# Memory norm's row scale applied to the products instead of the rows, memory rows loaded in column pieces, identity transposes left out

## The reference, cut to what matters

```python
def rms_norm(x, g):
    xf = x.astype(jnp.float32)
    y = xf * lax.rsqrt(jnp.mean(xf * xf, axis=-1, keepdims=True) + RMS_EPS)
    return (y * g.astype(jnp.float32)).astype(x.dtype)

mem_n = rms_norm(mem, mem_norm_g)              # mem: (256, 2048)
for layer in range(DEPTH):                     # DEPTH = 2
    mem_kv = mem_n @ mem_w_kv[layer]           # (2048, 1024): 512 columns of k, 512 of v
```

## Time and profile before

| | |
|---|---|
| median of three runs | 2245.72 us |
| profiled execution, span | 2243.6 us |
| TensorE busy | 2210.5 us (99%) |
| VectorE, ScalarE, GpSimd busy | 46%, 37%, 18% |
| TensorE idle ahead of its first instruction | 8.44 us |
| first product | 13.77 us |
| first product of memv0, memk1, memv1 | 40.47, 62.26, 88.92 us |

### The profile page before, as it was taken

How to read it: one execution, slowest core, us unless ns; L and a number is a source line. 1 busy time by engine, 2 the same in 40 slices (tenths; PEclk the granted TensorE clock), 3 DMA queues, 4 the chain that set the end, 5 groups by cost and what they waited for, 6 DMA issues and landing times.

```text
span 2243.6 us, 30418 instructions
## 1 busy us (share of the span) xinstructions
PE 2210.5 (99%) x11723; PEld 1824.8 (81%) x11723; DVE 1022.6 (46%) x1909; ACT 824.6 (37%) x1481; POOL 408.8 (18%) x699
## 2 busy tenths in 40 slices
PE   8999999999999999999999999999999999999998
PEld 7888888888888788888888878888887878777886
DVE  5632456556532356643353441442112357666534
ACT  6532233333323444422342223322222455555323
POOL 1626112322221012200010111100000154221100
PEclk9999999999999999999999999999999999999999
DMA  8645444444446346563353447444533675554632
GB/s 292 202 141 135 127 130 122 130 147 124 119 120 199 114 138 223 172 218 97 113 165 106 143 150 232 131 132 146 160 112 98 200 234 183 174 183 148 213 98 94
DMA packets 167052, 345.65 MB, mean 154 GB/s; under 512 B 21663, under 2 KB 32239, under 8 KB 164483
## 3 DMA queue, kind: packets, MB, share of 16 engines
q1 hardware_dynamic: 106832, 188.51, 28.1%
q0 software_dynamic: 31376, 98.44, 13.6%
q10 hardware_dynamic: 28707, 56.84, 6.9%
HBM read 279.89 MB, written 63.83 MB: 153 GB/s over the span
## 4 chain that ended last, share of the span: by engine, by line
PE 96%; ACT 1%; issue 1%; DVE 1%; DMA 1%; POOL 0%; SPq 0%; ACTq 0%; DVEq 0%; POOLq 0%
PE PS L244 79%; PE PS L1841 3%; PE PS L1830 2%; PE PS L296 1%; PE PS L2012 1%; PE PS L2367 1%; PE PS L587 1%; PE PS L1574 1%; PE PS L2541 1%; PE PS L2156 1%; PE PS L2400 1%; PE PS L2543 1%; PE PS L2037 1%; PE PS L658 1%; ACT wsp L206 0%
## 5 line engine op out<-in xcount | busy, mean ns | idle before, releaser
L244 PE MATMUL PS<-A,wsp 128*128 128x512 f32 (+2 forms) x5136 | 1141.0, 383 | 2.7 <-DVE A L573 1.2
L244 PEld LDWEIGHTS PS<-A,wsp 128*128 128x128 f32 (+1 forms) x5136 | 933.8, 188 | 196.5 <-issue 6.8
L213 DVE TENSOR_TENSOR wsp<-wraw,wsp 128x1024 fp32r<-128x1024 f32 (+1 forms) x357 | 431.3, 1209 | 889.4 <-ACT wsp L206 888.3
L244 PE MATMUL PS<-wsp,A 128*128 128x512 f32 x2928 | 747.5, 400 | 3.7 <-DVE stage L1912 1.8
L206 ACT ACTIVATE wsp<-wraw 128x1024 fp32r<-128x1024 f32 (+1 forms) x357 | 372.0, 1045 | 898.8 <-PE PS L244 868.2
L244 PEld LDWEIGHTS PS<-wsp,A 128*128 128x128 f32 x2928 | 531.8, 188 | 105.9 <-issue 9.4
L349 ACT ACTIVATE stage<-PS 128x512 f32<-128x512 f32 (+1 forms) x150 | 85.8, 592 | 104.3 <-PE PS L244 99.8
L1877 ACT ACTIVATE S<-PS 128x256 f32<-128x256 f32 (+3 forms) x160 | 63.0, 394 | 118.9 <-PE PS L1830 118.1
L1885 ACT ACTIVATE S<-PS,stats 128x256 f32<-128x256 f32 (+3 forms) x160 | 75.0, 469 | 75.8 <-DVE stats L1922 64.3
L1841 PEld LDWEIGHTS PS<-S 128*128 128x128 f32 x640 | 93.0, 191 | 10.2 <-issue 1.1
L1841 PE MATMUL PS<-S 128*128 128x128 f32 x640 | 94.3, 274 | 0.6 <-issue 0.6
(11 more groups left out here) (370 smaller groups left out, 1763.9 us busy)
## 6 DMA issues: line engine op xcount, KB each, us to landing
wraw<-in_even_w_in_dram SPq DMA_DIRECT2D x112, 512.0 KB, 3.7
wraw<-in_odd_w_in_dram SPq DMA_DIRECT2D x88, 512.0 KB, 3.6
wraw<-in_w_out_dram SPq DMA_DIRECT2D x80, 512.0 KB, 3.7
wraw<-in_mem_w_kv_dram SPq DMA_DIRECT2D x32, 512.0 KB, 4.3
yO<-stage ACTq DMA_DIRECT2D x12, 1024.0 KB
yE<-stage ACTq DMA_DIRECT2D x10, 1024.0 KB
S<-yO POOLq DMA_DIRECT2D x36, 256.0 KB, 3.7
hA<-stage ACTq DMA_DIRECT2D x8, 1024.0 KB
```

Source lines behind the costliest of these rows:

```text
L213: nc.vector.tensor_tensor(wsp[:, q, 1, :, 0:j["cols"]], wraw[:, q, :, 0:j["cols"]], wsp[:, q, 0, :, 0:j["cols"]].bitcast(F32), ALU.subtrac ...
L244: mm = nc.tensor.matmul(dst, lhs, rhs, start=(s == 0 and kk == 0 and i == 0), stop=(s == j["spc"] - 1 and kk == 1 and i == 2))
```

## The change

Six things change, all in the first 115 us.

- The rows of `mem` are transposed as they are loaded, without a scale. The row factor `memR` is applied when the products leave PSUM: for memv0 and memv1 by ScalarE, as the scale of its copy (`act_evac_cols`), and for memk0 and memk1, where a row is a column of the result, by VectorE, which multiplies with a tile `memB` that has the 256 factors in every partition (`dve_evac_rows`). `memB` is made by two matmuls of a matrix of ones with two diagonal matrices (`dve_diag`, `pe_row_scales` in slot 7 between its 12th and 13th product, `dve_row_scales`).
- The squares of `mem` move behind the tiles of slots 3 and 4, the root behind those of slot 5.
- `mem` is loaded in five column pieces of both row tiles (256, 256, 512, 512 and 512 columns), each ahead of one weight slot.
- The gains are loaded by ScalarE's queue at its start instead of by POOL's.
- The 14 identity transposes are left out.
- The loads of x tiles 2 and 3 wait for the sixth transposed k tile; those of tiles 0 and 1 for the squares as well.

`dve_evac_rows` stands in VectorE's queue where `act_evac` stood in ScalarE's: in the next product, behind the splits of its first three slots. ScalarE keeps the store there, which waits for the four banks.

```diff
-        def dve_chunk(dve, j, c, hook=None, split=0):
+        def dve_chunk(dve, j, c, hook=None, split=0, pending=None):
             for s, n, q, r, early in chunk_slots(j, c):
+                if s == 3 and pending:
+                    pending()
                 if s >= split:
                     dve_slot(dve, j, n, q)
...
+        def dve_evac_rows(dve, j):
+
+            if j["stored0"]:
+                dve.wait_ge(stored, 16 * j["stored0"])
+            for f in range(4):
+                dve.wait_ge(*((bank_done, j["done0"] + f + 1) if f < 3 else (slot_used, j["slot0"] + j["spc"])))
+                dve.wait_ge(rb_ok, 1)
+                nc.vector.tensor_tensor(stage[:, f, 0:NMEM], PS[:, f, 0:NMEM], memB, ALU.mult).then_inc(banks_free, 1)
+
+        def act_evac_cols(act, j):
+
+            act.wait_ge(stored, 16 * j["stored0"])
+            act.wait_ge(rows_ok, 1)
+            for f in range(2):
+                act.wait_ge(*((bank_done, j["done0"] + 1) if f < 1 else (slot_used, j["slot0"] + j["spc"])))
+                nc.scalar.activation(stage[:, f, :], PS[:, f, :], ACT.Copy, scale=memR[:, f:f + 1]).then_inc(banks_free, 1)
+            act_store(act, j, 0)
...
+        def dve_diag(dve):
+
+            for t in range(2):
+                nc.vector.tensor_scalar(diagS[t], ident[:, :], memR[:, t:t + 1], None, ALU.mult).then_inc(diag_ok, 1)
+
+        def pe_row_scales(pe):
+
+            pe.wait_ge(diag_ok, 2)
+            pe.wait_ge(const_ok, 1)
+            for t in range(2):
+                mm = nc.tensor.matmul(PS[:, 4, P * t:P * t + P], ones[:, :], diagS[t], start=(t == 0), stop=(t == 1))
+            mm.then_inc(rb_pe, 1)
+
+        def dve_row_scales(dve):
+            dve.wait_ge(rb_pe, 1)
+            nc.vector.tensor_copy(memB, PS[:, 4, 0:NMEM]).then_inc(rb_ok, 1)
+
         def pe_tile(pe, v, k):

+            if v["k"] == 0 and k in MEM_AT:
+                pe.wait_ge(mem_in[MEM_AT[k]], 16)
...
-        def pe_warm(pe):
-
-            for _ in range(14):
-                nc.tensor.transpose(PS[:, 1, 0:P], ident[:, :], ident[:, :])
...
+                if s == 7:
+                    pe_row_scales(pe)
                 pe_part(pe, j, 0, s, n, q, free, 0, 12, 24)
...
-            for t in range(2):
-                sp.dma_start(hrows[:, t, :], mem[t * P:(t + 1) * P, :]).then_inc(mem_in[t], 16)
-            for j in plan:
+            for s, n, q, r, early in chunk_slots(plan[0], 0):
+                if s < 5:
+                    sp.dma_start(hrows[:, 0:2, MEM_PIECES[s]], mem.rearrange("(t p) d -> p t d", p=P)[:, :, MEM_PIECES[s]]).then_inc(mem_in[s], 16)
+                sp_slot(sp, plan[0], 0, s, n, q, r, early, None)
+            for j in plan[1:]:
...
-            pool.wait_ge(sq_act, 2)
+            nc.gpsimd.memset(ones[:, :], 1.0).then_inc(const_ok, 1)
+            pool.wait_ge(nt_pe, 6)
...
+            for i, g in enumerate((a["norm_g"][0], a["norm_g"][1], a["mem_norm_g"])):
+                act.dma_start(gnat[KD * i:KD * i + KD, :], g.rearrange("(k p) -> k p", p=P)).then_inc(gains_in, 16)
             act_sqrt_ahead(act)
-            act_square(act, NORMS[0], 0)
-            act_square(act, NORMS[0], 1)
-            act_root(act, NORMS[0])
+            act_tiles(act, NORMS[0], (0,))
             act_first(act)
-            act_scale(act, NORMS[0], 1, FIRST)
-            act_tiles(act, NORMS[0], (0, 1))
-            act_scale(act, NORMS[0], 1, SECOND)
+            act_tiles(act, NORMS[0], (1,))
             act_split(act, plan[0], 1)
-            act_scale(act, NORMS[0], 1, THIRD)
             act_tiles(act, NORMS[0], (2, 3))
...
-            pend = lambda: act_evac(act, plan[0], 0)
+            pend = lambda: act_store(act, plan[0], 0)
             for n_, j in list(enumerate(plan[:4]))[1:]:
                 act_chunk(act, j, 0, pend, lambda s: act_early(act, n_, s))
-                pend = lambda j=j: act_evac(act, j, 0)
+                pend = lambda j=j: act_store(act, j, 0) if j["mode"] == "F" else act_evac_cols(act, j)
...
+            dve_tiles(dve, NORMS[0], (0,))
             dve_first(dve, 0)
+            dve_tiles(dve, NORMS[0], (1,))
             dve_first(dve, 1)
...
+                if s in (3, 4):
+                    dve_square(dve, s - 3)
+                if s == 4:
+                    dve_var(dve, NORMS[0])
+                if s == 5:
+                    dve_rms(dve, NORMS[0])
+                    dve_diag(dve)
+            dve_row_scales(dve)
             for n_, j in list(enumerate(plan[:4]))[1:]:
-                dve_chunk(dve, j, 0, lambda s: dve_early(dve, n_, s))
+                dve_chunk(dve, j, 0, lambda s: dve_early(dve, n_, s), pending=(lambda: dve_evac_rows(dve, plan[n_ - 1])) if n_ % 2 else None)
```

More of the change, by code:

```diff
@@ L107, in build @@
         gains_pe, gains_ok = sem("gains_pe"), sem("gains_ok")
+        const_ok = sem("const_ok")
         gnat = S[0:3 * KD, 16256:16384]
         rows_in = [sem(f"rows_in{t}") for t in range(4)]
-        mem_in = [sem(f"mem_in{t}") for t in range(2)]
+        MEM_PIECES = [slice(0, 256), slice(256, 512), slice(512, 1024), slice(1024, 1536), slice(1536, 2048)]
+        MEM_AT = {0: 0, 2: 1, 4: 2, 8: 3, 12: 4}
+        mem_in = [sem(f"mem_in{i}") for i in range(5)]
+        diag_ok, rb_pe, rb_ok = sem("diag_ok"), sem("rb_pe"), sem("rb_ok")
         scale_dve, scale_act = sem("scale_dve"), sem("scale_act")
@@ L397, in build @@
         sqp = sb("sqp", [P, 4, 4])
+        tC = sb("tC", [P, 512])
+        memB, diagS = tC[:, 0:NMEM], [tC[:, 256 + 128 * t:384 + 128 * t] for t in range(2)]
+        memR = small[:, 48:50]
         spare = sb("spare", [P, 1])
@@ L408, in act_square @@
             if v["k"] == 0:
[L409 to L412, removed]
+                for n in range(3):
+                    act.wait_ge(mem_in[n], 16)
+                nc.scalar.activation(S[:, 8192 + 1024 * i:9216 + 1024 * i], hrows[:, i, 0:D // 2], ACT.Square,
+                                     accum_out=small[:, i:i + 1]).then_inc(sq_act, 1)
                 return
@@ L422, in dve_square @@
         def dve_square(dve, t):
-            dve.wait_ge(mem_in[t], 16)
+            for n in (3, 4):
+                dve.wait_ge(mem_in[n], 16)
             half = hrows[:, t, D // 2:D]
@@ L448, in act_tile @@
                                  scale=gcol[:, v["g"], k:k + 1]).then_inc(nt_hi, 1)
-        FIRST, SECOND, THIRD, FOURTH, REST = slice(0, 256), slice(256, 512), slice(512, D), slice(512, 1024), slice(1024, D)
+        FOURTH, REST = slice(512, 1024), slice(1024, D)
         def scaled_rows(v, t, cs):
@@ L455, in act_scale @@
         def act_scale(act, v, t, cs):
-            if v["k"] == 0 and cs is FIRST:
-                act.wait_ge(rows_ok, 1)
             o, i, r = scaled_rows(v, t, cs)
@@ L555, in dve_rms @@
             ssq, var, root, r0, r1, r = (small[:, 4 * i:4 * i + t] for i in range(6))
+            if v["k"] == 0:
+                r = memR
             dve.wait_ge(rms_sqrt, v["k"] + 1)
@@ L580, in pe_tile @@
                 pe.wait_ge(scale_dve, by_dve)
-                pe.wait_ge(scale_act, by_act)
+                if by_act:
+                    pe.wait_ge(scale_act, by_act)
             g = norm_index(v, k)
@@ L588, in pe_tile @@
             mm.then_inc(nt_pe, 1)
-        SCALED = {(0, 0): (1, 1), (0, 2): (2, 2), (0, 4): (3, 3), (1, 0): (7, 3), (2, 4): (13, 5), (2, 8): (13, 9)}
-        def pe_warm(pe):
-            for _ in range(14):
-                nc.tensor.transpose(PS[:, 1, 0:P], ident[:, :], ident[:, :])
+        SCALED = {(1, 0): (4, 0), (2, 4): (10, 2), (2, 8): (10, 6)}
         def pe_norm(pe, v, j):
@@ L623, in pe_half_tiles @@
         def pe_half_tiles(pe, h):
-            pe.wait_ge(scale_dve, 8 + h)
-            pe.wait_ge(scale_act, 4 + h)
+            pe.wait_ge(scale_dve, 5 + h)
+            pe.wait_ge(scale_act, 1 + h)
             for k in range(4):
@@ L1436, in build @@
         identR = sb("identR", [P, P], F32R)
+        ones = sb("ones", [P, P])
         masknegR = sb("masknegR", [P, P], F32R)
@@ L2062, in build @@
         cols = sb("cols", [P, 16])
-        ones = sb("ones", [P, P])
-        const_in, const_ok = sem("const_in"), sem("const_ok")
+        const_in = sem("const_in")
         OFF = [0, 160, 448, 864]
@@ L2084, in pool_consts @@
             pool.dma_start(pec[:, :, :], a["nsa_cmp_pe"][0].rearrange("k l d -> d k l")).then_inc(const_in, 16)
-            nc.gpsimd.memset(ones[:, :], 1.0).then_inc(const_ok, 1)
             nc.gpsimd.memset(cm01[:, :], 1.0).then_inc(const_ok, 1)
@@ L2094, in pool_t5_loads @@
             pool.wait_ge(h1_out, 16)
-            pool.wait_ge(scale_dve, 13)
-            pool.wait_ge(scale_act, 9)
+            pool.wait_ge(scale_dve, 10)
+            pool.wait_ge(scale_act, 6)
             pool.dma_start(poskI, a["positions"].broadcast_to([P, T])).then_inc(t5_in, 16)
@@ L2649, in _ @@
         def _(pool):
-            for i, g in enumerate((a["norm_g"][0], a["norm_g"][1], a["mem_norm_g"])):
```

(14 more changed lines are left out.)

13 lines of the change are left out of this document (2 added, 11 removed).

## The result

The changed kernel takes 2251.58 us (median of 10 runs, 2248.78 to 2253.03) beside 2245.88 for the kernel before in the same runs. The ratio is 1.0024 (95% interval 1.0016 to 1.0032): 5.7 us slower, in a range of 3.6 to 7.2. I had forecast 2247.8 with a range up to 2251.0. The direction of the sum was right, its size was not: some 2 us were forecast, and the median lies 0.6 us above the range.

The account below looks back on a forecast made before the run. TensorE, busy 2210.5 of 2243.6 us, was taken as the bound. Terms -7.15 + 2.5 + 0.3 + 3.25 + 0.85 + 0.15 = -0.1, or +2.0 with a clock fall at memv0, gave 2247.8 us; range 2243.8 to 2251.

Parts of the forecast that it names:

- The first product: Start of TensorE's products in slot 0: at 6.9 instead of 13.77, 6.9 us earlier.
- the landing of the gains: Gain loads on ScalarE's queue at the start: 2.5 us from issue, there at 4.1; the other end was 7.4.
- the third rival: Gains land late at the start, at 7.4, sharing DMA engines with other loads; first product at 9.8, time 2250.7; 7 in 100.
- the landing of the slot: First weight slot (0.52 MB), issued by SP at 1.25: there at 5.1.
- The half rate behind the start: First products without identity transposes: 5.2 us at half clock rate lose 2.5 us (2.1 to 3.1).
- The first handover: memk0 to memv0: TensorE idle 3.25 us (2.5 to 3.8) while VectorE copies, does three splits, then the first multiply.
- The fall in that gap: Clock falls in TensorE's idle time ahead of memv0: +2.1 us, floor 1.0; 7 in 10.
- The second handover: memk1 to memv1: TensorE starts at 89.8 instead of 88.92, +0.85 us; idle grows from 1.14 to 2.0.
- the second fall: Rival: the clock falls at memv1 as well as memv0, +2.1 us more, to 2250 (2252 with high prices); 13 in 100.
- Loads, slots 3 to 5, the ones: Nothing waits for loads; VectorE's added work in slots 3 to 5 costs 0, at most +0.6; two ones matmuls +0.3.
- Sum up to E0: All terms of the change up to memv1: -0.1 us with the clock up, +2.0 with the clock falling at memv0.
- Behind 1700 us: Part after memv1: no term forecast; a changed length of the stretch behind memv1 would show the prediction wrong.

Follow-up runs that it names:

- the run with the one gain first: Against the mended kernel: ScalarE's queue loads the memory norm's gain first, only it is waited for, other two gains turned in slot 6; 2240.87 us.
- The filled gap: Changed kernel plus 24 identity transposes behind memk0, while TensorE waits for VectorE's first multiply; 2248.52 us, ratio 1.0010.
- first handover mended: Changed kernel with the two ones matmuls in slot 6 and memk0's multiplies behind one split instead of three; 2246.11 us, ratio 0.9998.
- the mended kernel: Changed kernel with ones matmuls in slot 6, memk0's multiplies behind one split and memk1's behind two, instead of three; 2243.66 us, ratio 0.9986.

## Why the prediction missed

**The first product: the step that failed.** I had it at 6.9, it came at 9.09. The working behind the landing of the gains was right to 0.1 us (2.8 us from the last gain to the first product as priced, 2.9 in the trace). The term that failed was the landing. I took 2.5 us from issue, near the row of 24 KB on SP; the third gain took 4.2, and its issue came at 1.81, not 1.6, since each issue on ScalarE took 0.47.

```profile
S<-in_norm_g_dram ACTq DMA_DIRECT2D x2, 8.0 KB, 3.3
S<-in_mem_norm_g_dram ACTq DMA_DIRECT2D x1, 8.0 KB, 4.2
```

The row of 2.1 us was taken from 1690 us on, where little was loaded (DMA share 0.11 from 1700 to 1720); the row on POOL, 5.8, stood beside the loads of mem, as the new issues do. The truth lay between. It was the third rival's mechanism in part, and it had a price (each us beyond 4.3 costs one) and a chance of 7 in 100, too low. The start gained 4.7 us instead of 6.9.

The gains don't account for all of the 2.2. In the run with the one gain first they are there at 4.02, as I had it, and the first product still comes at 7.66, because the first weight slot lands at about 6.1 (5.7 in the changed kernel), not at 5.1. So of the 2.2 us the gains' landing is worth about 1.4, and a second term, the landing of the slot, stood behind it with about 0.8.

**The half rate behind the start: right, its price a little high.** Priced at 2.5; slot 1 begins at 14.9, 2.7 before the old 17.62, where the start had gained 4.7 and a wait of 0.28 went: 2.2 lost. It lasted 5.5 us from the first product, 5.2 were priced. What was too high is the loss in each: I had said that products at half rate stand at least twice 0.12 apart, but they stand 0.213 apart (2.98 less a tail of 0.42, over 12):

```profile
11.58 2.98 PE L248 MATMUL PS<-A,wsp 128*128 128x256 f32 x13
```

In the kernel before, the same cost 1.4 to 1.7. It also differs between executions of one program: from the first product to the second stretch of slot 1 the three traces of the changed kernel take 6.9, 7.0 and 6.3 us.

**The first handover: right, as worked out.** 3.25 of idle predicted, 2.91 found, where the trace counts the idle time from the end of the last product and I had counted from where its successor could have begun. From the start of slot 7 to memv0 6.45 was predicted, and 6.4 are in the trace. VectorE's queue is the list of the prediction, item by item: the stand until the matmuls (2.88), the copy (0.42), three splits (3.49), the multiply. The run with the matmuls in slot 6 shows that the stand was its larger part.

**The fall in that gap: right.** Chance 7 in 10, price 2.1, measured 1.7 (memv0's 96 products take 23.64 beside 21.95). The price was that of 4.3 us at half rate, and it lasted 3.4. The filled gap shows that the idle time is the cause.

**The second handover: the wait right, its fall left out.** The wait is 1.99 as predicted (2.0), 0.85 more than before. The second fall stood as a rival at 13 in 100, and it came, in all three traces of the kernel, for 1.6 us (4.57 beside 2.98 in the first). The number of this rival, 2250 to 2252, was the right one, but by luck: the late start and the part behind 1700 us, which it didn't hold, made up for prices that were too high.

**Loads, slots 3 to 5, the ones: right.** I had 0 for VectorE's added work there; the slots take 3.3 us each as before. The two matmuls cost 0.36, priced at 0.3.

**Sum up to E0**: predicted +2.0, found +4.9 (5.3 and 4.3 in the repeats). The late first product gives +2.2 of this difference and the second fall +1.6; the cheaper half rate at the start, the cheaper first fall and the shorter gap take back 0.9.

**Behind 1700 us: open.** I had 0 there, and had named a change of length behind memv1 as a sign of being wrong. The first trace is 2.0 us longer than that of the kernel before, the repeats of the changed kernel 1.2 and 1.9, the seven experiments built on it 1.2 to 2.1, the kernel before without transposes 1.3, with 20 of them 0.5, its own repeat 0.4. So all ten traces with the change are longer there by more than the kernel before differs from its own repeat (0.4). That speaks against mere scatter, but two traces of the kernel before are few. What differs are waits such as this one, 0.3 in the first trace of the kernel before, 1.8 in the third of the changed kernel:

```profile
PE PS L2082 <- DMA S<-kmD: 1.8, 1, 1.8
```

The medians neither show nor exclude it: 5.7 and 4.4 us between the kernels in two groups of runs, against 4.3 to 5.3 up to E0. What decides it, and whether some of it belongs to the change, wasn't settled.

The range ended 0.6 us short of the median. With the landing's other end and the second fall in one case it would have had to reach 2253.

## What to carry to other kernels

When an evacuation moves to another engine, walk that engine's queue from its last free moment to the new instruction, and put the new instruction where its data come ready; here the same work gained 2.9 us over the kernel before or lost 5.7, by its place. An idle gap of 2 to 3 us in a steady stream of products costs its length and then up to 1.7 us of slow products, so count the clock with the wait; and identity transposes cost nothing while TensorE waits, and are worth more if they cover the whole wait (2.3 us here, against 1.4 to 1.7). A small load issued among large ones at the start is not priced by the fastest row of its size: here it took 4.2 us, between that row (2.1) and the one with large loads beside it (5.8).

## What was not expected of the hardware

- The same gap of 1.99 us ahead of memv1 was followed by 3.4 us at half clock in three traces of the changed kernel and by none in three other kernels (matmuls in slot 6, first handover mended, gap filled). So what the chip does with a gap this short depends on more than its length; on what wasn't settled. In all six traces it fell at memv1 where it had fallen at memv0 and only there; no run separates whether the one brings the other.
- Three small loads issued one after the other on ScalarE's queue landed in about 2.6, 4.0 and 4.2 us. A first one, alone needed, let TensorE start at 4.02.
- In the traces the identity transposes were worth 2.3 us in the mended kernel, where they fill nearly all of TensorE's idle start, and 1.4 to 1.7 in the kernel before (medians: 3.3 to 3.9, and 1.9).
